# Low parts of three of seven weight blocks by a negated copy and an accumulating DMA

## The reference

```python
def rmsnorm(x, g):
    x32 = x.astype(jnp.float32)
    y = x32 * lax.rsqrt(jnp.mean(x32 * x32, axis=-1, keepdims=True) + EPS)
    return (y * g.astype(jnp.float32)).astype(x.dtype)

def swiglu_ffn(h, w_in, w_out):
    gate, up = jnp.split(jnp.einsum('bsd,df->bsf', h, w_in), 2, axis=-1)
    return jnp.einsum('bsf,fd->bsd', jax.nn.silu(gate) * up, w_out)

h = h + rmsnorm(mixed, norm_gains[layer, 1])
hn = rmsnorm(h, norm_gains[layer, 2])
h = h + rmsnorm(swiglu_ffn(hn, ffn_w_in[layer], ffn_w_out[layer]), norm_gains[layer, 3])
```

## Time and profile before

| what | value |
|---|---|
| median of 3 runs | 2322.84 us (2322.04 to 2323.28) |
| span of the profiled execution, first to last instruction | 2320.9 us |
| median of the runs minus that span | 1.9 us |
| TensorE busy | 2309.1 us (99%) |
| VectorE busy | 1498.3 us (65%) |
| ScalarE busy | 1119.0 us (48%) |
| GpSimd busy | 223.6 us (10%) |
| HBM read | 221.28 MB |

### The profile page before, as it was taken

The page is one execution under the profiler, slowest core; times in us unless marked ns, Lnnn a source line. Parts: engine busy times, 40 slices in busy tenths (PEclk is TensorE's granted clock), DMA queues, the critical chain, the costliest instruction groups (busy, mean ns, idle before and its releaser), DMA issues.

```text
span 2320.9 us, 32131 instructions
## 1 busy us (share of the span) xinstructions
PE 2309.1 (99%) x12088; PEld 1950.9 (84%) x12088; DVE 1498.3 (65%) x2173; ACT 1119.0 (48%) x1829; POOL 223.6 (10%) x313
## 2 busy tenths in 40 slices
PE   9999999999999999999999999999999999999999
PEld 8777889988888888999888778888888878888887
DVE  6665789952738968899428876777434456777731
ACT  6655544452539965445326854444323444544420
POOL 1221013200125410232000000000001000000000
PEclk9999999999999999999999999999999999999999
DMA  5433223332242222333322223323322323233232
GB/s 167 152 132 102 85 92 109 104 112 93 87 118 64 64 84 82 99 110 111 113 89 77 64 82 91 100 90 106 100 93 91 100 69 95 91 100 100 95 107 79
DMA packets 72541, 226.30 MB, mean 98 GB/s; under 512 B 7921, under 2 KB 19489, under 8 KB 72417
## 3 DMA queue, kind: packets, MB, share of 16 engines
q1 hardware_dynamic: 67840, 210.72, 28.5%
q0 software_dynamic: 4576, 13.89, 1.9%
HBM read 221.28 MB, written 2.18 MB: 96 GB/s over the span
## 4 chain that ended last, share of the span: by engine, by line
PE 92%; DVE 3%; ACT 3%; POOL 1%; issue 1%; DMA 0%; DVEq 0%; ACTq 0%; SPq 0%
PE bank L338 26%; PE bank L340 25%; PE bank L339 25%; PE bank L478 5%; PE bank L470 4%; PE bank L1605 1%; PE bank L1596 1%; PE bank L1639 1%; DVE w_lo L312 0%; DVE h L756 0%; POOL hgrn_lv L2560 0%; PE bank L2651 0%; PE bank L2015 0%; POOL hgrn_lv L2547 0%; PE bank L3103 0%
## 5 line engine op out<-in xcount | busy, mean ns | idle before, releaser
L312 DVE TENSOR_TENSOR w_lo<-raw,w_hi 128x1024 fp32r<-128x1024 f32 (+1 forms) x310 | 402.3, 1308 | 218.4 <-ACT w_hi L307 218.1
L338 PE MATMUL bank<-x_hi,w_hi 128*128 128x512 f32 x1344 | 529.2, 394 | 1.2 <-ACT sb_q L2761 1.0
L340 PE MATMUL bank<-x_hi,w_lo 128*128 128x512 f32 x1344 | 523.4, 389 | 0.0
L339 PE MATMUL bank<-x_lo,w_hi 128*128 128x512 f32 x1344 | 523.1, 389 | 0.0
L307 ACT ACTIVATE w_hi<-raw 128x1024 fp32r<-128x1024 f32 (+1 forms) x310 | 344.6, 1121 | 179.9 <-PE bank L340 93.5
L338 PEld LDWEIGHTS bank<-x_hi,w_hi 128*128 128x128 f32 x1344 | 252.3, 188 | 57.4 <-issue 3.1
L340 PEld LDWEIGHTS bank<-x_hi,w_lo 128*128 128x128 f32 x1344 | 252.2, 188 | 53.0
L339 PEld LDWEIGHTS bank<-x_lo,w_hi 128*128 128x128 f32 x1344 | 252.5, 188 | 51.2 <-issue 0.5
L338 PE MATMUL bank<-st_a_hi,w_hi 128*128 128x512 f32 (+1 forms) x396 | 145.1, 366 | 0.0
L340 PE MATMUL bank<-st_a_hi,w_lo 128*128 128x512 f32 (+1 forms) x396 | 144.7, 365 | 0.0
L1374 DVE TENSOR_TENSOR bank<-bank,rstd 128x512 f32<-128x512 f32 x120 | 83.2, 696 | 92.2 <-PE bank L340 92.2
(11 more groups left out here) (444 smaller groups left out, 4673.2 us busy)
## 6 DMA issues: line engine op xcount, KB each, us to landing
raw<-in_w_up SPq DMA_DIRECT2D x120, 512.0 KB, 3.5
raw<-in_w_down SPq DMA_DIRECT2D x64, 704.0 KB, 4.2
st_raw_even<-in_w_up SPq DMA_DIRECT2D x28, 512.0 KB, 4.2
st_raw_odd<-in_w_up SPq DMA_DIRECT2D x24, 512.0 KB, 4.0
raw<-in_w_fox_qk SPq DMA_DIRECT2D x16, 512.0 KB, 3.7
raw<-in_w_hgrn_qf SPq DMA_DIRECT2D x16, 512.0 KB, 3.5
fox_c_keys_a<-fox_c_rows POOLq DMA_DIRECT2D x8, 640.0 KB, 4.1
fox_c_keys_b<-fox_c_rows POOLq DMA_DIRECT2D x8, 640.0 KB, 4.5
```

The lines of the kernel that those rows point to most:

```text
L312: nc.vector.tensor_tensor(w_lo[:, slot, 0:size], raw[:, slot % 2, 0:size], w_hi[:, slot, 0:size].bitcast(F32), ALU.subtract).then_inc(sem( ...
L338: nc.tensor.matmul(out, w[0], x[0], start=first, stop=False)
L339: nc.tensor.matmul(out, w[0], x[1], start=False, stop=False)
L340: return nc.tensor.matmul(out, w[1], x[0], start=False, stop=last)
```

## The change

The low parts of a and g are no longer made by VectorE. ScalarE writes, behind the high part, its negative to the place of the low part (it computes the copy of the raw block once more, with scale -1). Then GpSimd issues a DMA that reads the raw block from HBM again and adds it there: raw minus high. Two semaphores count ScalarE's negatives, four count the landings (a and g, even and odd pairs). `st_lo` counts three low parts a pair instead of five. TensorE waits for the landing of a ahead of part 0 as before for its low part, and for that of g ahead of part 6 only. On GpSimd the DMA of a for pair 0 stands ahead of all sums; then, for each pair n, sums, DMA of g of pair n, DMA of a of pair n+1.

```diff
@@ -928,16 +931,17 @@
             if not n:
                 pe.wait_ge(sem("st_xlo"), 7 * f + 7)
             pe.wait_ge(sem("gated_ready"), FT * f + (ST_FIRST + n - 2 if n > 1 else 5 + 2 * n) + 1 + 2)
-            pe.wait_ge(sem("st_lo"), 5 * g + 1)
+            wait(pe, f"st_added_a{g % 2}", 16 * (g // 2) + 16)
             part(0, acc[0]).then_inc(sem("st_part"), 1)
             part(1, acc[1])
-            pe.wait_ge(sem("st_lo"), 5 * g + 2)
+            pe.wait_ge(sem("st_lo"), 3 * g + 1)
             part(2, acc[2]).then_inc(sem("st_part"), 1)
             part(3, acc[3])
-            pe.wait_ge(sem("st_lo"), 5 * g + 3)
+            pe.wait_ge(sem("st_lo"), 3 * g + 2)
             part(4, acc[4]).then_inc(sem("st_part"), 1)
-            pe.wait_ge(sem("st_lo"), 5 * g + 5)
+            pe.wait_ge(sem("st_lo"), 3 * g + 3)
             part(5, acc[5])
+            wait(pe, f"st_added_g{g % 2}", 16 * (g // 2) + 16)
             part(6, acc[6]).then_inc(sem("unit_used"), 2)
@@ -1100,6 +1104,8 @@
             nc.scalar.activation(st_w(n, 0, at), src, ACT.Copy).then_inc(sem("st_hi"), 1)
+            if blocks in ("a", "g"):
+                nc.scalar.activation(st_w(n, 1, at), src, ACT.Copy, scale=-1.0).then_inc(sem("st_minus_" + blocks), 1)
@@ -1238,21 +1244,34 @@
+        def rest_by_dma(pool, f, n, blocks):
+
+            g = ST_PAIRS * f + n
+            unit = io[f"w_up{f}"][2 * (ST_FIRST + n) + (blocks == "g")].rearrange("p (b x) -> p b x", b=2)
+            src, at = (unit, slice(0, 2)) if blocks == "a" else (unit[:, 1:2, :], slice(6, 7))
+            wait(pool, "st_minus_" + blocks, g + 1)
+            pool.dma_start(st_w(n, 1, at), src, accum_op=ALU.add).then_inc(sem(f"st_added_{blocks}{g % 2}"), 16)
+
         def pool_ffn(pool, s):
             f = s // 2
+            if f < 2:
+                rest_by_dma(pool, f, 0, "a")
             for n in range(ST_PAIRS if f < 2 else 0):
...
                 nc.gpsimd.tensor_tensor(st_third[:, 0, :], ra[:, 0, :], rg[:, 0, :], ALU.add).then_inc(sem("st_pool"), 1)
+                rest_by_dma(pool, f, n, "g")
+                if n < ST_PAIRS - 1:
+                    rest_by_dma(pool, f, n + 1, "a")
@@ -1321,7 +1339,6 @@
                 if more:
-                    dve_pair(dve, f, n + 1, "a")
                     dve_sums(dve, f, n + 1, False)
@@ -1330,7 +1347,6 @@
                     dve_pair(dve, f, n + 1, "s3")
-                    dve_pair(dve, f, n + 1, "g")
                     dve_cross(dve, f, n, 1)
@@ -1393,7 +1409,6 @@
                             dve_pair(dve, f, 0, "s3")
-                            dve_pair(dve, f, 0, "g")
                             dve_pair(dve, f, 0, "s4")
@@ -1431,7 +1446,6 @@
                         dve_form_lo(dve, f, 6)
-                        dve_pair(dve, f, 0, "a")
                         dve_sums(dve, f, 0, False)
```

More of the change, by code:

```diff
@@ L139, in build @@
             "sb_scores": ("st_part", 3 * ST_ALL), "sb_prob": ("st_first", ST_ALL), "sb_beta": ("st_hi", 5 * ST_ALL), "sb_pooled": ("st_pool", 2 * ST_ALL),
-            "sb_turned": ("st_lo", 5 * ST_ALL), "sb_pt": ("st_sum", 2 * ST_ALL), "sb_pv": ("st_cross", 4 * ST_ALL),
+            "sb_turned": ("st_lo", 3 * ST_ALL), "sb_pt": ("st_sum", 2 * ST_ALL), "sb_pv": ("st_cross", 4 * ST_ALL),
             "sb_fail": ("st_form", 10), "sb_cum": ("st_xhi", 14), "sb_phi": ("st_xlo", 14),
@@ L144, in build @@
             "gla_min": ("fx_setup", 4), "gla_abs": ("fx_ls", 3),
+            "st_minus_a": ("fx_gate_out", 1), "st_minus_g": ("fx_gate_sum", 1),
+            "st_added_a0": ("fx_keys_0", 16 * FOX_PAIRS), "st_added_a1": ("fx_keys_1", 16 * FOX_PAIRS),
+            "st_added_g0": ("fx_rows", 16 * TT), "st_added_g1": ("fx_gate_low", 16),
         }
@@ L1247, in pool_ffn @@
                 if n:
-                    pool.wait_ge(sem("st_lo"), 5 * (g - 1) + 2)
+                    pool.wait_ge(sem("st_lo"), 3 * (g - 1) + 1)
                 else:
@@ L1253, in pool_ffn @@
                 if n:
-                    pool.wait_ge(sem("st_lo"), 5 * (g - 1) + 3)
+                    pool.wait_ge(sem("st_lo"), 3 * (g - 1) + 2)
                 nc.gpsimd.tensor_tensor(st_third[:, 0, :], ra[:, 0, :], rg[:, 0, :], ALU.add).then_inc(sem("st_pool"), 1)
+                rest_by_dma(pool, f, n, "g")
+                if n < ST_PAIRS - 1:
+                    rest_by_dma(pool, f, n + 1, "a")
         def dve_sums(dve, f, n, second):
@@ L1264, in dve_sums @@
                 if n:
-                    dve.wait_ge(sem("st_lo"), 5 * g)
+                    dve.wait_ge(sem("st_lo"), 3 * g)
                 nc.vector.tensor_tensor(st_sum[:, 0, :], st_sum[:, 1, :], ra[:, 0, :], ALU.add).then_inc(sem("st_sum"), 1)
             else:
-                dve.wait_ge(sem("st_lo"), 5 * g + 2)
+                dve.wait_ge(sem("st_lo"), 3 * g + 1)
                 dve.wait_ge(sem("st_sum"), 2 * g + 1)
@@ L1275, in dve_pair @@
             ra, rg = st_raw_pair(n)
-            src, at, count = {"a": (ra, slice(0, 2), 1), "s12": (st_sum[:], slice(2, 4), 2),
-                              "s3": (st_third[:], slice(4, 5), 3), "g": (rg[:, 1:2, :], slice(6, 7), 4),
+            src, at, count = {"s12": (st_sum[:], slice(2, 4), 2), "s3": (st_third[:], slice(4, 5), 3),
                               "s4": (st_sum[:, 0:1, :], slice(5, 6), 5)}[blocks]
@@ L3401, in _ @@
                         elif n:
-                            sp.wait_ge(sem("st_lo"), 5 * (ST_PAIRS * f + n - 1))
+                            sp.wait_ge(sem("st_lo"), 3 * (ST_PAIRS * f + n - 1))
                         for i in range(2):
@@ L3411, in _ @@
                     for i in range(2):
-                        sp.wait_ge(sem("st_lo"), 5 * (ST_PAIRS * f + ST_PAIRS - 1 + i))
+                        sp.wait_ge(sem("st_lo"), 3 * (ST_PAIRS * f + ST_PAIRS - 1 + i))
                         sp.dma_start(raw[:, i, 0:ph.size], io["w_" + name][i]).then_inc(sem(f"raw_ready{i}"), 16)
```

## The result

| | before | after |
|---|---|---|
| median of 4 runs each | 2322.77 us (2322.04 to 2323.28) | 2341.38 us (2339.25 to 2342.27) |
| ratio, 95% interval | | 1.008 (1.0065 to 1.0094) |
| profiled execution, span | 2320.9 us | 2337.5 us |

The change makes the kernel 18.6 us slower; the two profiled executions differ by 16.6 us. 1.6 us was forecast. The granted clock is 1.00 in the rows of both, so none of the 16.6 us is the clock.

A forecast was written before the change was run, and what follows sets the result against it. TensorE's matmuls were taken as the bound, with helpers slightly ahead. VectorE's relief counted 0 and pair 1's wait 2 x 0.8 = +1.6 us, giving 2324.4 us; forecast's own range 2322 to 2327, full range 2321.5 to 2344.

The forecast's parts named there:

- VectorE loses 26.6 us a stage ... worth 0: VectorE drops 28 low parts a stage, 26.6 us; TensorE waited for none of them, so nothing is gained.
- I take 0.6: Time GpSimd's queue is held for one adding DMA issue: 0.6 us, ends 0.57 and 1.15.
- The loop of 9.88 us: Chain per pair from DMA issue through GpSimd, VectorE and ScalarE to the next issue: 9.88 us, against TensorE's 10.09.
- the 0.2 us a pair: Lead the helpers' loop was to gain on TensorE each pair, so that TensorE waits only once a stage.
- the threshold of 0.8 us for an issue: Issue time on GpSimd above which TensorE would run at the loop's pace: 0.6 + 0.21 = 0.8 us.
- Between 5.1 and 6.5 I take 6.0: Landing of block a's 512 KB add: 5.1 us alone, at most 1.4 more beside a raw load; 6.0 taken.
- price 0: Pair 0's block a: the DMA has 6.9 us to land and takes 6.0, so TensorE loses nothing.
- Pair 1 "waits 0.8 us": Pair 1's block a has 5.2 us to land and takes 6.0, so TensorE waits 0.8 us once a stage.
- Block g "0": Pair 0's last block: half the data has 6.5 us to land before part 6, so it costs nothing.
- Rival "the loop becomes the bound": TensorE runs at the helper loop's pace if issues exceed 0.8 us; +11 us at 1.15 us; chance 0.22.
- its best witness: One copy's issue of 0.79 us at 93.21, evidence for long issues, put down to VectorE's one-input ops beside it.
- Rival "the add is slow": Above 6.9 us to land, pair 0 waits too; at 10 us, 7 us a stage, +14 us; chance 0.21.

The follow-up runs named there:

- e4_no_dma: The change without its DMAs: TensorE waits for ScalarE's negative, and the raw blocks are never added; 2322.02 us, ratio 0.9999 to the kernel before.
- e2_copy: The change with GpSimd's DMAs as plain copies in place of adds, queue order kept; 2328.74 us, ratio 1.0028 to the kernel before.
- e8_alone: The change with SyncE's two raw loads of pair 1 held until pair 0's adding DMA of block a has landed; 2339.15 us, ratio 1.0075.
- e6_a_only: The change with only block a's low part by ScalarE and adding DMA, block g's by VectorE as before; 2340.77 us, ratio 1.0078.
- e5_g_only: The change with only block g's low part by ScalarE and adding DMA, block a's by VectorE as before; 2329.11 us, ratio 1.0035.
- e1_reorder: The change with GpSimd's order turned: the next pair's first sum stands ahead of the DMA of a; 2330.92 us, ratio 1.0036.
- e11_g_between: Block g alone by adding DMA, with GpSimd's next first sum ahead of that DMA and its second sum behind; 2322.01 us, ratio 0.9997.
- e12_two_by_vector: The change with GpSimd's order turned (sum, DMA of g, sum, DMA of a) and block a of each stage's first two pairs by VectorE; 2336.15 us, ratio 1.0058.
- e7_short_add: The change with each added DMA cut to the first 16 columns of each row of a block; 2346.86 us, ratio 1.0105.
- e3_reorder_copy: The change with GpSimd's order turned (next pair's first sum ahead of the DMA of a) and plain copies for adds; 2324.14 us, ratio 1.0009.
- e10_two_issues: The change with block a's add issued as two DMAs of 256 KB instead of one of 512 KB; 2366.22 us, ratio 1.0189.

## Why the prediction was right or wrong

The time of 2341.38 us lies in the range given (to 2344), but not in the forecast's own (2322 to 2327), and 18.6 us were lost where 1.6 were forecast. Both rivals on the slow side came true together, each in a mild form; that their sum still fell inside a range drawn for one of them at a time is in part luck.

- **"VectorE loses 26.6 us a stage ... worth 0", ScalarE's copies hidden**: right, shown by e4_no_dma (24.8 us less and 19.0 more a stage, for 26.6 and 23.5). The DMA share of 0.77 was right too: 0.78.
- **"I take 0.6" for the issue**: the first step that failed. It takes 0.87 to 0.91; the ends given were 0.57 and 1.15. I took it from copies, and e2_copy shows 0.53 for a copy in this very place. I also read the copies' rows wrongly: 0.79 was not there "once" but in 4 of the 16 issues of 640 KB, and two more took 0.65.
- **The loop of 9.88 us**: every step was the right one. Measured 10.41: 0.33 from the issue, 0.18 from handing ScalarE's negative over to the DMA (0.30, where I took 0.12), the rest within 0.04 a step. With 0.57 for the issue it is 10.07 (e2_copy), so the 0.2 us a pair that I counted as gained each time wasn't there even so, and the threshold of 0.8 us for an issue was too high: with the handing over as measured the margin is used up at 0.53.
- **"Between 5.1 and 6.5 I take 6.0" for the landing**: the second failed step. The 5.1 alone was right (5.3, e8_alone), and so was the data time counted twice: the add alone moves 209 GB/s where raw loads moved 414. The Trainium skill's rule ("Collectives: The Full Stack", The bandwidth ceiling), told there of collectives, that an add inside the DMA halves the rate because it needs two source reads, agrees with this. What was too small is the sharing: I gave at most 1.4 us to the raw loads, measured 2.8 at pair 0 (8.1 against 5.3). Pair 0 was reckoned with the same 6.0, though I had named the two raw loads issued at 325.2 beside it, so its "price 0" became 1.3 us.
- **Pair 1 "waits 0.8 us"**: 1.12, with the a-DMA issued at 337.08 and landed in 7.0. It would have been more had pair 0's delay not moved the need as well.
- **Block g "0"**: right in the change (e6_a_only). e5_g_only shows that this hangs on the queue's order.
- **Rival "the loop becomes the bound"**: at 0.87 its own rule gives 9.88 + 0.32 - 10.09 = 0.11 us over, 1.3 us a stage on 12 pairs; with the handing over it became 0.33. The issue is long because of its kind, not of its neighbours: copies in the same place take 0.53. At 337.08 it reads 0.87 while VectorE does nothing (busy 0.00 in 337:338). So what the Trainium skill says of neighbours ("SBUF — State Buffer", Who interferes with whom), that two-input VectorE adds leave GpSimd's descriptor writing alone, was no ground to take "its best witness" from this rival. The trace of before doesn't speak against the rule: the six of 16 copies' issues that took 0.65 or 0.79 all stand beside VectorE's TENSOR_SCALARs, with one tensor input, the ten of 0.57 to 0.58 beside others.
- **Rival "the add is slow"**: its landing of 8.2 us lies over the 6.9 from which pair 0 waits. "Later pairs don't wait" was wrong, as the loop ate their lead.
- **Sharing out the 18.6 us**: loop 10.5, adding against copying 6.8, a copy's landing 1.8 (the differences of the medians; they make 19.0 against the medians of before taken beside the experiments). By e1_reorder's trace some 1.5 us of the 6.8 belong to its clock, and so to the loop's side.

The mistake behind both is one: two small margins, 0.2 us a pair and 0.9 us at pair 0, were each judged with a mid value of an unmeasured cost, and the sum counted only the one wait that came out over zero. No version beat the kernel before: e11_g_between equals it, and so does e4_no_dma, which leaves the adding out.

## What to carry to other kernels

A DMA put into the queue of an engine that computes is an instruction of that engine: follow the chain from it round to itself, and if it comes within a few per cent of the bound engine's period, the price is paid every time round, however few the bytes. Put such an issue behind the work that others wait for, not ahead of it (10.5 us here, 7.1 for block g alone). When a relief is worth nothing because the bound engine never waits, any added link in the helpers' chain can only cost. And look at the granted clock behind every long wait of TensorE before a difference of a few microseconds is given to a mechanism.

## What the runs showed of the hardware

- An adding DMA issued by GpSimd holds it 0.87 to 0.91 us (the first of the second stage 0.98, and about 1.2 as read where it directly follows a sum, in e1_reorder and e12_two_by_vector), a plain one of the same shape 0.53 to 0.57, one of 256 rows of 64 bytes 1.07 to 1.14, one of 128 such rows 0.89 (e7_short_add). The sums behind an adding issue read 1.62 us instead of 1.29.
- 512 KB added: 5.3 us alone, 7.0 to 9.0 in the change, with 1 MB of raw loads a pair; 256 KB about 4.0. As a copy: median 5.6 in the change's order, 4.1 in e3_reorder_copy; 256 KB 2.8.
- The add alone moves 209 GB/s at a full share (342:343 in the change).
- TensorE's granted clock fell to 0.50 for 3.4 or 6.8 us in six of the experiments (e1, e6, e7, e8, e10, e12), each time during or just behind a wait of 1.8 to 5.3 us. Not every such wait did it: two of 2.4 and 2.6 us in e10_two_issues passed at 1.00. In the two stages of the change, whose longest wait is 1.6 us, it never fell.
- A VectorE subtraction of 128x512 that starts beside GpSimd's sums is held until they are through: 1.78 us beside one, 3.79 beside two in a row, 0.68 without. I had counted such a meeting in the loop, but not that two sums in a row hold VectorE up for both.
